# Inverting the chunk triangles of an RWKV-7 layer: moving the 16x16 diagonal blocks by TensorE turns and masked copies instead of DMAs through DRAM

## What is computed

```python
def step(S, inp):
    r_t, w_t, k_t, v_t, kk_t, a_t = inp
    sa = jnp.einsum('bhvk,bhk->bhv', S, kk_t)
    S = (S * w_t[:, :, None, :]
         - sa[..., None] * (kk_t * a_t)[:, :, None, :]
         + v_t[..., None] * k_t[:, :, None, :])
    y = jnp.einsum('bhvk,bhk->bhv', S, r_t)
    return S, y
...
proj = jnp.einsum('sbtd,sde->sbte', xs, w_in)
r, k, v, g = proj[0], proj[1], proj[2], proj[3]
...
return (y * jax.nn.silu(g)) @ w_out
```

## Time and profile before

| what | value |
|---|---|
| median of 3 runs | 2498.12 us (2497.87 to 2498.51) |
| the profiled execution | 2493.24 us, span 2491.5 us |
| mean granted clock of TensorE | 0.983 |
| busy: TensorE, VectorE, ScalarE, POOL | 2387.5, 1510.5, 1184.3, 19.1 us |
| gate projection with the inversion | about 332 to 501 us of the span |

### The profile page before, as it was taken

One profiled execution on the slowest core, in us unless ns is written; L12 is line 12 of the kernel. 1 busy time (PEld: TensorE's weight loads), 2 busy tenths in 40 slices (PEclk: granted clock), 3 DMA queues, 4 the chain that ended last, 5 costly groups with the idle time before them and its releaser, 6 DMA issues.

```text
span 2491.5 us, 49242 instructions
## 1 busy us (share of the span) xinstructions
PE 2387.5 (96%) x20449; PEld 2274.2 (91%) x20449; DVE 1510.5 (61%) x1825; ACT 1184.3 (48%) x1496; POOL 19.1 (1%) x35
## 2 busy tenths in 40 slices
PE   8999996987999999999999999999999999999997
PEld 7999996977999899999899998999999888999886
DVE  7577556657664455656789895554955444555444
ACT  5676352134454456654653345356544433444342
POOL 0000000000000000000000000000000000000000
PEclk9999998998999999999899999999999999999999
DMA  8355567314545554455456564556566555666554
GB/s 274 120 177 170 178 194 178 95 39 170 178 159 185 187 178 147 150 189 177 138 175 178 162 186 152 176 163 187 161 202 176 187 187 185 186 184 186 186 186 135
DMA packets 233940, 425.06 MB, mean 171 GB/s; under 512 B 33680, under 2 KB 36064, under 8 KB 233040
## 3 DMA queue, kind: packets, MB, share of 16 engines
q1 hardware_dynamic: 207232, 397.46, 51.2%
q10 hardware_dynamic: 23872, 12.82, 2.2%
q0 software_dynamic: 2656, 12.17, 1.6%
HBM read 413.48 MB, written 8.91 MB: 170 GB/s over the span
## 4 chain that ended last, share of the span: by engine, by line
PE 86%; DVE 7%; ACT 3%; issue 2%; DMA 1%; ACTq 0%; DVEq 0%; SPq 0%; POOL 0%
PE ps L492 26%; PE ps L493 26%; PE ps L494 26%; PE ps L703 2%; DVE wlo L352 2%; ACT whi L348 1%; PE ps L711 1%; PE ps L622 1%; PE ps L608 1%; DVE regions L1798 0%; DVE act_lo L1991 0%; PE ps L891 0%; ACT regions L1409 0%; ACTq L1233 0%; ACT L1409 0%
## 5 line engine op out<-in xcount | busy, mean ns | idle before, releaser
L352 DVE TENSOR_TENSOR wlo<-wraw,whi 128x1024 fp32r<-128x1024 f32 x752 | 918.3, 1225 | 888.3 <-ACT whi L348 887.3
L492 PE MATMUL ps<-act_hi,whi 128*128 128x256 f32 (+1 forms) x4736 | 1356.6, 286 | 43.3 <-DVE act_lo L2102 12.7
L493 PE MATMUL ps<-act_lo,whi 128*128 128x256 f32 (+1 forms) x4736 | 1340.9, 283 | 0.0
L494 PE MATMUL ps<-act_hi,wlo 128*128 128x256 f32 (+1 forms) x4736 | 1339.3, 283 | 0.0
L348 ACT ACTIVATE whi<-wraw 128x1024 fp32r<-128x1024 f32 x752 | 794.6, 1060 | 1119.1 <-PE ps L494 1074.2
L492 PEld LDWEIGHTS ps<-act_hi,whi 128*128 128x128 f32 x4736 | 899.7, 190 | 49.7 <-issue 30.2
L493 PEld LDWEIGHTS ps<-act_lo,whi 128*128 128x128 f32 x4736 | 902.4, 191 | 1.1
L494 PEld LDWEIGHTS ps<-act_hi,wlo 128*128 128x128 f32 x4736 | 899.6, 190 | 0.0
L494 PE MATMUL ps<-whi,regions_r 128*128 128x512 f32 x512 | 203.0, 396 | 0.0
L493 PE MATMUL ps<-wlo,regions_r 128*128 128x512 f32 x512 | 203.0, 396 | 0.0
L492 PE MATMUL ps<-whi,regions_r 128*128 128x512 f32 x512 | 203.0, 396 | 0.0
(11 more groups left out here) (316 smaller groups left out, 1393.7 us busy)
## 6 DMA issues: line engine op xcount, KB each, us to landing
wraw<-in_a_w_in SPq DMA_DIRECT2D x128, 512.0 KB, 3.9
wraw<-in_w_up SPq DMA_DIRECT2D x128, 512.0 KB, 3.9
wraw<-in_w_down SPq DMA_DIRECT2D x128, 512.0 KB, 4.3
wraw<-in_w_in SPq DMA_DIRECT2D x112, 512.0 KB, 3.8
wraw<-in_b_w_qg SPq DMA_DIRECT2D x64, 512.0 KB, 3.7
wraw<-in_a_w_out SPq DMA_DIRECT2D x32, 512.0 KB, 3.6
wraw<-in_w_k_shared SPq DMA_DIRECT2D x32, 512.0 KB, 4.5
wraw<-in_w_v_shared SPq DMA_DIRECT2D x32, 512.0 KB, 4.5
```

The costliest lines, as they stand in the source:

```text
L352: nc.vector.tensor_tensor(wlo[:, q % RING], wraw[:, q % RING], whi[:, q % RING].bitcast(F32), ALU.subtract).then_inc(lo_ready, 1)
L492: mm(o, hi_s, hi_m, start=first, stop=False, skip_group_check=True)
L493: mm(o, hi_s, lo_m, start=False, stop=False, skip_group_check=True)
L494: i = mm(o, lo_s, hi_m, start=False, stop=last, skip_group_check=True)
```

## The change

Steps 2 and 4 no longer go through DRAM.

- *Gather.* VectorE packs each chunk's diagonal blocks with a mask per partition (`pack_ab`, four operations: the partition's own 16 of 64 columns are kept). TensorE turns the packed tile by 32 matmuls with the identity (kind "gather"): turn t takes every 16th column as weights, and puts tokens in the free direction and head and chunk in the partitions. ScalarE copies the result from ps to `diag` (`take_blocks`), reading neighbours that lie 64 elements apart.
- *Scatter.* The same 32 matmuls on `inv` (kind "scatter"), and four masked copies by ScalarE from ps into TTs (`place_blocks`), with the same stride; they write zeros outside the diagonal, so POOL's memsets of TTs go. One mask of 4 columns joins the constants.
- *Order.* The coefficient products stand at half slabs 0, 4, 5, 7 (before 0, 4, 6, 8) and alternate between banks 6, 7 and 4, 5; the gather turn is at half slab 10, the scatter turn at 31, the substitution at VectorE's slabs 5 to 13 (before 8 to 16), `first_turn` of chunk 0 at slab 16 (before 21), and the level products begin at half slab 35 and are spread over 28 half slabs, up to 62, where they stood in pairs on 44 to 59. `store_ab` and `load_ab` stay, since the levels still read the coefficients from DRAM. The buffers AB, Tm and Yl change places.

```diff
+    parts["blocks"] = (s // 16 == np.arange(4)[None, :]) * 1.0
...
-        TAKE_AT = (0, 2, 3, 4)
+        AB_AT, TAKE_AT, AB_BANK = (0, 4, 5, 7), (0, 2, 2, 3), (6, 4, 6, 4)
         for c in range(4):
-            steps_at[2 * TAKE_AT[c]] = [("ab", c, 0, 0), ("ab", c, 1, 0)]
-        for n_, (c, lv, kind) in enumerate((c, lv, kind) for c in range(4) for lv in (4, 5) for kind in "yz"):
-            for f in range(2):
-                steps_at[44 + n_] += [(kind, c, f, lv)]
-        SUBSTITUTE_AT = {8: range(1, 6), 9: (6, 7), 10: (8, 9), 11: (10,), 12: (11,), 13: (12,), 14: (13,), 15: (14,), 16: (15,)}
+            steps_at[AB_AT[c]] = [("ab", c, 0, 0), ("ab", c, 1, 0)]
+        steps_at[10] = [("gather", 0, 0, 0)]
+        steps_at[31] = [("scatter", 0, 0, 0)]
+        for n_, (c, lv, kind, f) in enumerate((c, lv, kind, f) for c in range(4) for lv in (4, 5) for kind in "yz" for f in range(2)):
+            steps_at[35 + 7 * n_ // 8] += [(kind, c, f, lv)]
+        SUBSTITUTE_AT = {5: range(1, 6), 6: (6, 7), 7: (8, 9), 8: (10,), 9: (11,), 10: (12,), 11: (13,), 12: (14,), 13: (15,)}
...
+                if kind == "gather":
+                    pe.wait_ge(S["bvs_ready"], 4)
+                    pe.wait_ge(S["ab_packed"], 4)
+                    for t in range(16):
+                        for p in range(2):
+                            m_ = mm(ps[side(p), 6 + t // 8, cols(t % 8)], packed_ab[side(p)].rearrange("p c q t -> p (c q) t")[:, :, t],
+                                    cs("ident64")[side(p), :], start=True, stop=True)
+                    m_.then_inc(S["blocks_mm"], 1)
+                if kind == "scatter":
+                    pe.wait_ge(S["inv_ready"], 1)
+                    pe.wait_ge(S["blocks_ready"], 1)
+                    for t in range(16):
+                        for p in range(2):
+                            m_ = mm(ps[side(p), 6 + t // 8, cols(t % 8)], inv[side(p)].rearrange("p b s t -> p (b s) t")[:, :, t],
+                                    cs("ident64")[side(p), :], start=True, stop=True)
+                    m_.then_inc(S["blocks_mm"], 1)
...
                 if kind == "z":
                     pe.wait_ge(S["lv_ysb"], m_ + 1)
                     if m_ < 2:
-                        pe.wait_ge(S["inv_loaded"], 128)
-                        pe.wait_ge(S["bvs_ready"], 4)
+                        pe.wait_ge(S["blocks_ready"], 5)
...
-            def gather_ab():
-                act.wait_ge(S["bv_stored0"], 32)
+            def take_blocks():
+
+                act.wait_ge(S["blocks_mm"], 1)
+                st.do(a(diag.rearrange("p b s t -> p (b s) t"), bank(6, 2).rearrange("p (t s) -> p s t", t=16), ACT.Copy), sig["blocks_ready"])
+
+            def place_blocks():
+
+                act.wait_ge(S["blocks_mm"], 2)
                 act.wait_ge(S["ab_stored"], 128)
                 for b in range(4):
-                    bs = slice(16 * b, 16 * b + 16)
-                    act.dma_start(diag[:, b], ab_dram[bs].rearrange("s p c q n -> (p c q) s n")[:, :, bs]).then_inc(S["ab_gathered"], 16)
+                    st.do(a(TTs.rearrange("p c (q n) -> p (c q) n", n=N)[:, :, 16 * b:16 * b + 16], bank(6, 2).rearrange("p (t h) -> p h t", t=16),
+                            ACT.Copy, scale=cs("blocks")[:, b:b + 1]), sig["blocks_ready"])
...
-                    if t == 17:
-                        act.wait_ge(S["inv_ready"], 1)
-                        act.dma_start(inv_dram[:], inv).then_inc(S["inv_stored"], 16)
-                    if t == 18:
-                        act.wait_ge(S["inv_stored"], 16)
-                        act.wait_ge(S["zeroed"], 6)
-                        scatter(act)
+                    if t == 5:
+                        take_blocks()
+                    if t == 16:
+                        place_blocks()
...
+            def pack_ab(c):
+
+                if c == 0:
+                    dve.wait_ge(S["bv_stored0"], 32)
+                dve.wait_ge(S["ab_ready"], 2 * c + 2)
+                for b in range(4):
+                    x_, w_ = heads(TTs[:, c, :])[:, :, 16 * b:16 * b + 16], cs("blocks")[:, b:b + 1]
+                    if b:
+                        st.prev()
+                        st.do(stt(packed_ab[:, c], x_, w_, packed_ab[:, c], ALU.mult, ALU.add), sig["ab_packed"] if b == 3 else None)
+                    else:
+                        st.do(ts_(packed_ab[:, c], x_, w_, None, ALU.mult))
...
-                    if (s, u) == (2, 5):
+                    if (s, u) == (2, 0):
                         for f in range(2):
                             first_turn(0, f)
```

More of the change, by code:

```diff
@@ L258, in program @@
         TTs = R[:, 0, :].rearrange("p (c n) -> p c n", c=4)
-        AB, Tm, Yl = [R[:, 1, 1024 * i:1024 * (i + 1)] for i in range(2)], R[:, 1, 2048:3072], R[:, 1, 3072:4096]
+        AB, Tm, Yl = [R[:, 1, 3072 * i:3072 * i + 1024] for i in range(2)], R[:, 1, 2048:3072], R[:, 1, 1024:2048]
         blocks = lambda t_: t_.rearrange("p (b s t) -> p b s t", b=4, s=16)
         diag, inv, terms = blocks(Tm), blocks(Yl), R[:, 1, 0:1024]
+        packed_ab = Tm.rearrange("p (c q t) -> p c q t", c=4, q=HEADS // 2)
         AM = wk(0, 3072).rearrange("p (j a t) -> p j a t", j=KT, a=3)
@@ L370, in store_out @@
                 eng.dma_start(out.rearrange("o (b p) n -> p (o b) n", p=P)[:, tb, cols], Htok[:, tb, cols]).then_inc(S["out_stored"], 16)
[L373 to L378, removed]
         @block.sync
@@ L436, in _ @@
         def _(pool):
-            pool.wait_ge(S["bv_stored1"], 32)
-            nc.gpsimd.memset(inv, 0.0).then_inc(S["zeroed"], 1)
-            pool.wait_ge(S["zeroed"], 1)
-            nc.gpsimd.memset(Yl.rearrange("p (b n) -> p b n", b=4)[:, :, 0:256:17], 1.0).then_inc(S["zeroed"], 1)
             pool.wait_ge(S["rk_bc"], 4)
-            for c in range(4):
-                pool.wait_ge(S["ab_stored"], 128)
-                nc.gpsimd.memset(TTs[:, c, :], 0.0).then_inc(S["zeroed"], 1)
+            nc.gpsimd.memset(inv, 0.0).then_inc(S["inv_ones"], 1)
+            pool.wait_ge(S["inv_ones"], 1)
+            nc.gpsimd.memset(Yl.rearrange("p (b n) -> p b n", b=4)[:, :, 0:256:17], 1.0).then_inc(S["inv_ones"], 1)
             def load_ab(c):
@@ L676, in hook @@
                         m_.then_inc(S["vt_mm"], 1)
-                    if q == 3:
+                    if q == (4 if g == 3 else 3):
                         pe.wait_ge(S["rk_ready"], g + 1)
@@ L739, in level @@
                         pe.wait_ge(S["bcm_ready"], 4)
[L740 removed]
+                    into_tokens((f,), AB_BANK[c], key(Bc, c), chan(KR, 0, ts), sig=S["ab_mm"])
+                if kind == "gather":
[14 more added lines that the diff above has]
+                    m_.then_inc(S["blocks_mm"], 1)
                 if kind == "y":
@@ L1220, in take_ab @@
                     act.wait_ge(S["ab_mm"], 2 * c + f + 1)
-                    st.do(a(TTs[:, c, f * GW:(f + 1) * GW], bank((4 if c else 6) + f), ACT.Copy, scale=-1.0), sig["ab_ready"])
+                    st.do(a(TTs[:, c, f * GW:(f + 1) * GW], bank(AB_BANK[c] + f), ACT.Copy, scale=-1.0), sig["ab_ready"])
             def store_ab(c):
@@ L1237, in hook @@
                     t = 8 * s + u
[L1238 to L1251 removed]
+                    for c in range(4):
+                        if t == TAKE_AT[c]:
+                            take_ab(c)
+                            store_ab(c)
+                    if t == 4:
+                        bonus_store(3)
+                    if t == 5:
+                        take_blocks()
+                    if t == 16:
+                        place_blocks()
                 return hook
@@ L1831, in hook @@
                 def hook(u):
-                    if (s, u) == (0, 3):
+                    for c in range(4):
+                        if 8 * s + u == TAKE_AT[c]:
+                            pack_ab(c)
+                    if (s, u) == (0, 4):
                         bonus(3)
```

23 lines of the change are left out of this document (8 added, 15 removed).

## The result

| set | kernel before, us | changed kernel, us | ratio (95%) |
|---|---|---|---|
| first, 5 runs of each | 2497.87 (2495.62 to 2498.51) | 2484.37 (2481.93 to 2487.54) | 0.9949 (0.9937 to 0.9960) |
| again, on another chip | 2495.07 (2492.13 to 2496.33) | 2483.02 (2479.19 to 2486.93) | 0.9953 (0.9940 to 0.9967) |

The change is faster by 12 to 13.5 us, about 0.5%.

What follows compares the result with a forecast made beforehand. TensorE, busy 96% of the span, was taken as the bound; 24.3 us removed against 19.3 added gave net -5.0, so a median of 2493.1 us from 2498.12, range 2485 to 2500.

Steps and rivals of the forecast that it cites:

- The price of a stride: Five ScalarE copies from ps, neighbours 64 elements apart: 0.95 us more each, the upper bound; the lower was nothing.
- (e): TensorE's wait for place_blocks before the first level product: 3.2 us, 7.0 with the stride's price.
- (d): TensorE's wait for the inverse before the scatter turn: 1.6 us, 2.4 with the stride's price.
- rival A: PSUM strides are free: added 14.2, net -10.1 us, 2488.0; chance 0.30.
- (f): Strided weight loads of the two turns on TensorE: 0.5 us taken, bounds 0 and 10.7.
- rival C: The turns are slow, strided weight loads not overlapped: 10.7 us instead of 0.5, net +5.2, 2503.3; chance 0.12.
- (b): Level products on TensorE, spread as 4 pairs and 24 singles: 42.5 us against 39.4, so 3.2 more.
- rival D: The shorter wait, before the scatter turn, drops the clock too: 1.7 us more, net -3.3, 2494.8; chance 0.14.
- 24.3: Sum in us of TensorE's gate-projection waits and the slow clock behind them that the change removes.
- (a): The gather and scatter turns on TensorE, each 32 matmuls of 64x64: 4.1 us added for both.

Runs made afterwards that it cites:

- run 5: Run 4 with the packed tile stored t-major, so the gather turn's weights are neighbours: 2477.06 us, 0.9917 of the kernel before.
- run 6: Run 5 with the inverse stored t-major too, so both turns' weights are neighbours: 2475.51 us, 0.9911 of the kernel before.
- run 10: Run 6 with the gather turn at half slab 11 instead of 10: 2471.65 us, 0.9905 of the kernel before.
- run 3: Changed kernel with the level products in pairs on half slabs 44 to 59, not spread from 35: 2477.23 us, 0.9928 of the kernel before.
- run 12: The kernel before again, unaltered, with its own profile: 2493.93 us, ratio 0.9997.
- run 1: Kernel before with only the scatter replaced by a turn (half slab 41), gather still by DMAs: 2480.10 us, 0.9938 of the kernel before.
- run 8: Changed kernel with only the level products moved, from half slab 38 at three quarters of a half slab each: 2477.44 us, 0.9930 of the kernel before.
- run 11: The changed kernel again, unaltered, on another batch's chip: 2483.02 us, 0.9953 of the kernel before.
- run 7: Run 1 with the four gather DMAs issued by POOL instead of ScalarE: 2482.05 us, 0.9938 of the kernel before.
- run 4: Changed kernel with the scatter turn at half slab 32 and level products spread from 38: 2474.62 us, 0.9918 of the kernel before.
- run 9: Run 4 repeated beside run 8 and run 11 on one chip: 2477.18 us, 0.9929 of the kernel before.

## Why the prediction was right or wrong

**What it had right.** The sign, the place of every wait that went and of each of the three that came, and the arithmetic of both new waits before the price of a stride was put on them: 1.6 and 3.2 us without it, 1.84 and 3.20 measured. (The substitution starts 15.4 us earlier, at 367.19 against 382.58, where I said some 18; no term hung on it.) That the scatter's wait would shrink and not go was right, and so was what it hangs on (VectorE's substitution, which now ends at 395.04, and ScalarE's four copies). The load of the first coefficients cost nothing, as said.

**The step that failed: "The price of a stride".** I put 0.95 us on each of five copies from ps and took the upper bound, "being what the nearest rows show". Both rows read SBUF; one was another engine, the other an instruction of 64 elements. Measured: 1.007 us for a strided copy against 1.03 for a contiguous one, so nothing. That alone is 3.8 us in wait (e) and 0.8 in (d): 4.6 of the 5.1 us between the forecast and rival A. Rival A had the better argument. The sentence of the Trainium skill on matmuls with a non-contiguous access pattern ("Advanced Engine Details and Errata", Memory Cachelines) is not touched by this: it speaks of matmuls, and these reads are ScalarE's. The strided weights, which did slow TensorE, lie in SBUF, and that sentence stands under the lines of PSUM; it foretold neither.

**(f) was sized too low.** "I take 0.5, near the low end" for two turns; it is 2 x (3.76 - 1.91) = 3.7. Of that, 2 x (3.76 - 2.08) = 3.4 is the stride (runs 5, 6 and 10). That is rival C's cause at a lower price, without its premise that the loads don't overlap: 3.76 us for 64 loads is 59 ns a load, under the 75 from which C decides, and twice the 30 of a product (1.91 / 64). The recorded loads overlap in both (64 x 200 ns in 3.76 us, 64 x 135 ns in 1.91). The runs show the stride as the cause, not which part of the load sets the pace.

**(b) was sized too high.** 3.2 more for the spread levels by 1.38 a single; their starts are 2.69 apart on average, which less a half slab of 1.42 gives 1.27. 24 x 1.27 + 4 x 2.34 = 39.8, so 0.4 more. A single has hardly any change-over.

**The clock.** I counted 1.7 us behind (e) and none behind (d) in the forecast; rival D had it behind (d). In the profile it fell behind both; in 408 to 414 alone 5.04 busy us ran at 0.50, a loss of 2.5. But the wider finding is that such a wait can bring the loss and need not. Of nine waits of 1.5 to 1.9 us before 64x64 matmuls, four had a fall behind them (runs 3, 6 and 12, and the changed kernel's first profile) and five had none (runs 1, 5, 8 and 11, and the first profile of before). In run 7 it fell even behind one of 1.23. Behind the 2.16 or 2.17 us before the recurrence it fell in two of fourteen profiles, behind a 2.44 (run 7) not at all. I had taken single outcomes, a fall behind 2.67 and none behind 2.0, as a bound between waits that drop the clock and waits that don't. What decides between the two outcomes stays open here.

**The sum.** Terms as measured: turns 7.6, levels 0.4, waits 0.88 + 1.84 + 3.20, slow clock about 4 (in part it lies beside the turn, which is no slower for it: 3.81 against 3.76), in all some 18 against 19.3 forecast. That the recurrence is earlier by 7.9 and not by 24.3 - 18 leaves 1.6 us on the side of what was removed. The same 1.5 to 2 is left over in runs 4, 8 and 10. Part of it stands in the rows of before: behind each of its stalls the next half slab takes 1.52 us instead of 1.42. The rest I haven't assigned. Some sums of the prediction are also a little off by their own terms: (a) is 4.0 and not 4.1, (b) 3.1 and not 3.2, and C, at the 1.94 ns an element of rows 8 and not 1.8, 11.8 and not 10.7. None changes the order of the cases.

**Profile and median.** The prediction carried the 4.9 us between the profiled execution and the median over as a constant. Run 12 shows that it need not be one: an execution of before can have a loss of 3.4 us, at a place that the change removes, that the first profile happened not to have. How many of the executions have it isn't known. With it, rival A's sum would have given 2497.87 - 10.1 - 3.4 = 2484.4; that this is the measured median is luck in part, for errors cancel in it, (b) and (f) and the second fall of the clock among them.

## What to carry to other kernels

When a transfer's wait is removed, the next ones in the chain decide: move the consumers, here by one half slab and by three, until the timeline shows hardly a wait before them, since in this kernel that brought the recurrence 7.8 to 8.6 us further forward (runs 9 and 4; 5.8 in the medians of one chip), as much there as the change itself, and one line, the place of the level products, was most of it (run 8). Price a strided access from a row of the same engine, the same memory and a like size; where there is none, weigh both bounds evenly. And where the profiled execution isn't the median one, look for a wait whose clock loss may come and go before the gap is carried over as a constant.

## What the runs showed of the hardware

- ScalarE reads PSUM at a stride of 64 float32 as fast as contiguously: 1007 ns for 1024 elements a partition, 1107 with a mask as scale.
- 32 matmuls of 64x64 float32 take 3.76 us where the weights are 16 elements apart and 2.08 where they are neighbours (200 and 135 ns a recorded load).
- With its output of 256 elements 64 apart VectorE pays 97 ns more (350 to 447) in TENSOR_SCALAR; in SCALAR_TENSOR_TENSOR, where one input has the same stride, 243 (485 to 728). A second strided operand in the substitution's product costs little: 1756 ns for 900 elements in run 4, 1830 in run 6.
- Eight DMAs of small pieces hold ScalarE's queue for 11.8 to 14.7 us, four for 9.5 to 10.9; on POOL the four took 4.8.
- Behind a wait of 1.5 to 1.9 us before 64x64 matmuls the granted clock fell to 0.50 in four profiles, for a loss of 1.7 us in three and 3.4 in one (run 12), and stayed 1.00 in five; both kernels stand on either side. Behind the 2.16 or 2.17 us before the recurrence it fell in two of fourteen profiles (run 6 and the changed kernel's first).
